# First block's attention: where VectorE does a finished branch's product and sum, and when ScalarE copies the first factor

## The reference

```python
Kc = compress(kc_raw, pe_k, ck_w1, ck_w2)
Vc = compress(vc_raw, pe_v, cv_w1, cv_w2)
...
s_c = jnp.einsum('bgrtd,bgnd->bgrtn', qblk, Kc) - slope * dist_c
p_c = jnp.where(valid_c, jax.nn.softmax(jnp.where(valid_c, s_c, NEG), axis=-1), 0.0)
o_c = jnp.einsum('bgrtn,bgnd->bgrtd', p_c, Vc)
...
p_s = jax.nn.softmax(s_s, axis=-1).reshape(B, G, R, T, n_sel, SEL_BLOCK)
o_s = jnp.einsum('bgrtnl,bgtnld->bgrtd', p_s, Vsel)
...
p_w = jax.nn.softmax(jnp.where(valid_w, s_w, NEG), axis=-1)
o_w = jnp.einsum('bgrts,bgsd->bgrtd', p_w, vwin)
return gblk[..., 0:1] * o_c + gblk[..., 1:2] * o_s + gblk[..., 2:3] * o_w
...
x = x + jnp.concatenate([m_out, a_out], axis=-1) @ w_out[i]
x = x + conv_ffn(rms_norm(x, ln2_g[i]), w_up[i], conv_w[i], conv_b[i], w_down[i])
```

## Time and profile before

| | |
|---|---|
| median of 3 runs | 1676.45 us (1676.28 to 1678.82) |
| profiled execution | 1674.83 us, span 1673.5 us |
| mean granted TensorE clock | 0.985 |
| PE busy | 1606.2 us (96%), 10381 matmuls |
| DVE busy | 871.9 us (52%) |
| ACT busy | 633.4 us (38%) |
| POOL busy | 50.4 us (3%) |
| in 217 to 355 us: PE, DVE, ACT busy, clock | 121.06, 79.79, 75.54 of 138 us, 0.90 |

### The profile page before, as it was taken

The page is one execution under the profiler, slowest core; times in us unless marked ns, Lnnn a source line. Parts: engine busy times, 40 slices in busy tenths (PEclk is TensorE's granted clock), DMA queues, the critical chain, the costliest instruction groups (busy, mean ns, idle before and its releaser), DMA issues.

```text
span 1673.5 us, 24837 instructions
## 1 busy us (share of the span) xinstructions
PE 1606.2 (96%) x10381; PEld 1356.3 (81%) x10381; DVE 871.9 (52%) x1558; ACT 633.4 (38%) x1124; POOL 50.4 (3%) x51
## 2 busy tenths in 40 slices
PE   7999978999999999999999999999999998999997
PEld 5898766677888888899888778999987887678886
DVE  4434666556644655855454455436555445545443
ACT  5232256443322334733344342223333343442333
POOL 0000001000000000020000000000020000000000
PEclk9999989899999999999999899999999999999999
DMA  6234400024233322332112102223422113113231
GB/s 196 76 80 89 113 14 14 14 88 119 84 100 101 101 80 96 99 67 76 51 51 49 54 14 77 77 89 120 96 51 76 51 37 51 54 39 101 89 113 51
DMA packets 175600, 125.22 MB, mean 75 GB/s; under 512 B 48752, under 2 KB 172272, under 8 KB 175488
## 3 DMA queue, kind: packets, MB, share of 16 engines
q1 hardware_dynamic: 175488, 123.63, 26.5%
HBM read 121.52 MB, written 2.10 MB: 74 GB/s over the span
## 4 chain that ended last, share of the span: by engine, by line
PE 89%; DVE 4%; ACT 4%; issue 2%; DMA 1%; SPq 0%; POOL 0%; DVEq 0%; ACTq 0%; POOLq 0%
PE bank L586 69%; PE bank L2743 2%; PE bank L2775 2%; PE bank L2755 2%; PE bank L3151 1%; ACT w_hi L533 1%; PE bank L2651 1%; PE bank L2602 1%; PE bank L1602 1%; DVE w_lo L542 1%; PE bank L1658 1%; PE bank L3114 1%; PE bank L1478 1%; ACT probs L1532 1%; PE bank L3130 1%
## 5 line engine op out<-in xcount | busy, mean ns | idle before, releaser
L586 PE MATMUL bank<-h_hi,w_hi 128*128 128x512 f32 (+2 forms) x920 | 327.4, 376 | 7.6 <-issue 4.4
L542 DVE TENSOR_TENSOR w_lo<-w_raw,w_hi 128x2048 fp32r<-128x2048 f32 (+2 forms) x117 | 241.2, 2061 | 177.0 <-ACT w_hi L533 176.4
L586 PE MATMUL bank<-h_lo,w_hi 128*128 128x512 f32 (+2 forms) x920 | 322.6, 370 | 0.0
L586 PE MATMUL bank<-h_hi,w_lo 128*128 128x512 f32 (+2 forms) x920 | 321.2, 369 | 0.0
L533 ACT ACTIVATE w_hi<-w_raw 128x2048 fp32r<-128x2048 f32 (+2 forms) x117 | 201.1, 1719 | 74.4 <-DMA w_raw<-w_in 36.0
L586 PEld LDWEIGHTS bank<-h_hi,w_hi 128*128 128x128 f32 (+1 forms) x920 | 166.9, 189 | 49.9 <-issue 16.6
L586 PEld LDWEIGHTS bank<-h_hi,w_lo 128*128 128x128 f32 (+1 forms) x920 | 166.6, 189 | 30.6 <-issue 0.2
L586 PEld LDWEIGHTS bank<-h_lo,w_hi 128*128 128x128 f32 (+1 forms) x920 | 166.5, 189 | 30.1 <-issue 0.5
L586 PE MATMUL bank<-g_hi,w_hi 128*128 128x264 f32 (+1 forms) x752 | 183.0, 309 | 1.4 <-DVE z_a L2225 0.9
L586 PE MATMUL bank<-g_lo,w_hi 128*128 128x264 f32 (+1 forms) x752 | 180.8, 306 | 0.0
L586 PE MATMUL bank<-g_hi,w_lo 128*128 128x264 f32 (+1 forms) x752 | 180.4, 306 | 0.0
(11 more groups left out here) (574 smaller groups left out, 2633.1 us busy)
## 6 DMA issues: line engine op xcount, KB each, us to landing
w_raw<-w_in SPq DMA_DIRECT2D x45, 1024.0 KB, 5.3
w_raw<-w_up SPq DMA_DIRECT2D x32, 512.0 KB, 4.9
w_raw<-w_in SPq DMA_DIRECT2D x40, 256.0 KB, 4.5
w_raw<-w_down SPq DMA_DIRECT2D x8, 1024.0 KB, 5.1
w_raw<-w_out SPq DMA_DIRECT2D x8, 1024.0 KB, 5.1
w_raw<-w_out SPq DMA_DIRECT2D x8, 512.0 KB, 3.4
w_raw<-w_ple_gate SPq DMA_DIRECT2D x4, 1024.0 KB, 5.1
w_raw<-w_o_attn SPq DMA_DIRECT2D x8, 512.0 KB, 3.5
```

Of the source, the lines that this page charges most:

```text
L542: DV.e.tensor_tensor(wlo[u % RING][:, 0:n], raw[u % RING][:, 0:n], whi[u % RING][:, 0:n].bitcast(F32), ALU.subtract).then_inc(*w_low(u))
L586: ins = PE.e.matmul(out, stationary[a](k), moving[b](k)[i], start=first and n == 0, stop=last and n == 2)
```

## The change

Two edits. In `nsa_steps`, used by ScalarE and VectorE, the value part of unit step - 3 moves ahead of the step's fill. In `ac_nsa_turn` the copy of the first unit's factor (unit (0, 0, 0)) moves from the second unit's turn, at step 3, to the end of the first unit's own turn at step 2, behind its `ac_nsa_wide` and ahead of the exponentials of unit (0, 2, 0), which ScalarE does in the same step. TensorE's order is not changed.

```diff
@@ -1614,7 +1614,7 @@
         def ac_nsa_turn(unit):
             i = number_n[unit]
             dst, src = flip(unit, 0)
-            if i and is_last(units_n[i - 1]):
+            if i > 1 and is_last(units_n[i - 1]):
                 ac_nsa_factors(units_n[i - 1])
             if i > 1:
                 AC.wait_ge(*n_valued.at(i - 2))
@@ -1622,6 +1622,7 @@
             AC.e.activation(dst, src, ACT.Copy).then_inc(*n_flip_a(i, 0))
             if i == 0:
                 ac_nsa_wide(unit)
+                ac_nsa_factors(unit)
 
         def ac_nsa_widen(unit):
             i = number_n[unit]
@@ -1736,11 +1737,11 @@
                 for stage_, behind in stages_:
                     if 0 <= step - behind < len(units_n):
                         stage_(units_n[step - behind])
+                if step > 2:
+                    value(units_n[step - 3])
                 while given < 11 * min(step, len(units_n)) // len(units_n):
                     next(fill)
                     given += 1
-                if step > 2:
-                    value(units_n[step - 3])
 
         def ac_nsa():
             fence(AC, "mlstm")
```

## The result

| | before | after |
|---|---|---|
| median | 1676.45 us (3 runs: 1676.28, 1676.45, 1678.82) | 1663.05 us (4 runs: 1659.98, 1662.26, 1663.84, 1665.06) |
| ratio | | 0.9919, 95% interval 0.9899 to 0.994 |
| profiled execution, span | 1674.83, 1673.5 us | 1663.84, 1662.5 us |
| mean granted TensorE clock | 0.985 | 0.992 |

A fourth run of before was disturbed (3445.82 us) and is neither in the median nor in the ratio. By the ratio the change is faster by 0.8%, some 13.6 us (10 to 17); a second comparison of the same two kernels gave 10.8 us (experiment 5). The forecast of 1663.0 agrees with the median to 0.1 us. That is closer than its steps deserve: the stalls came out as worked out, the clock gave less, the first factor more, and what lies outside the stage differed too.

What follows compares the result with a forecast made beforehand. TensorE was taken as the bound, carrying 89% of the chain. Stalls 5.06, clock 7.8 and first factor 0.6 sum to 13.5 us off the profiled 1674.83; from the median 1676.45 that gives 1663.0 us, range 1658 to 1670.

Steps and rivals of the forecast that it cites:

- The order of the code: In nsa_steps, fill and finished branch meet on VectorE only at steps 15, 19 and 24; the swap acts nowhere else.
- B: Step 19, unit (2,2,3): TensorE's stall of 0.83 us goes; called the tightest spot of the three.
- Part 1: VectorE's product moves ahead of addition and split at three places; TensorE's stalls go, 5.06 us together.
- the prediction's last part: Signs expected in the trace after, among them w_lo still waiting for w_hi, with about 0.4 us.
- A: Step 15, unit (2,1,3): TensorE's stall of 2.28 us for the finished branch goes.
- C: Step 24, unit (3,1,3): TensorE's stall of 1.95 us for the finished branch goes.
- Part 2: TensorE's three low-clock stretches in or behind the stalls all go: 7.8 us, bounds 0 to 7.8.
- rival (a): A low-clock stretch stays or appears, or VectorE's probsT copy replaces B's wait: 1666 to 1669.2 us; chance 27%.
- Part 3: In the opening, ScalarE copies the first factor ahead of eight exponentials: 0.6 us gained, between +1.0 and -1.6.
- (b): Only the stalls go and every low-clock stretch lasts as now: 5.7 us gained, 1670.8 us; chance 8%.
- (c): VectorE's multiply is late in its new place and TensorE stalls elsewhere: 1674 to 1676.5 us; chance 4%.
- (d): Slower: shifted later TensorE gaps bring new low-clock stretches, 3.1 us each; five give 1678.5 us; chance 3%.

Runs made afterwards that it cites:

- experiment 5: The kernel after, unchanged, run once more against the kernel before: 1664.39 us, ratio 0.9933.
- experiment 4: Kernel before, with the branch's product and sum put between the dense step's addition to X and its split; first factor as before: 1666.83 us, ratio 0.9942.
- experiment 10: Kernel with late copies, and at B ScalarE's w_hi also held back behind that place's second factor: 1659.76 us, one execution.
- experiment 3: Kernel before, with 16, 6 and 14 useless identity transposes on TensorE ahead of its waits at A, B and C: 1670.47 us, ratio 0.997.
- experiment 2: Kernel before with only the earlier copy of the first factor, without the swap in nsa_steps: 1674.54 us, ratio 0.999.
- experiment 6: Kernel before with value ahead of the fill only at step 19 (place B): 1674.36 us, ratio 0.9996.
- experiment 7: Kernel after, with 4 to 8 more identity transposes on TensorE in each of its waits for a branch factor: 1664.96 us, ratio 0.9941.
- late copies: Kernel after, with ScalarE's first, second and fourth mLSTM fill copies held back behind the next step's branch factor: 1660.29 us, ratio 0.9909.
- experiment 1: Kernel after without the two edits in ac_nsa_turn, so the swap in nsa_steps alone: 1663.4 us, ratio 0.9928.

## Why the prediction was right, and where it was not

**The order of the code** (steps 15, 19 and 24 and no others): right. The dense step from X7 to X8, which has no finished branch beside it, stayed at 6.99 us, and the swap at B alone took away B's stall alone.

**Part 1, the stalls**: right in size and cause. 2.28 + 0.83 + 1.95 = 5.06 us were predicted; 2.34 + 0.96 + 2.03 = 5.33 measured. The cover named for the moved instructions, the wait for `w_hi`, is there, and it is the split that had held them up (experiment 4). Of it the prediction's last part expected 0.4 us to be left; measured were 0.24 us at B and nothing at A and C, so the cover is just used up, as its own starts (288.4 against 288.39) had said. The product's starts were given to 0.1 us against the stage. That B is the tightest place was right, and experiment 10 shows no slack there.

**Part 2, the clock**: the mechanism was right (experiment 3), and 7.8 us against 7.63 is right for the profiled execution of before. (The eight transposes from which the share of 0.46 comes are of 128x128 each, not of 128x512; the share stays.) Wrong was the step that took the clock as safe afterwards, with the patch of 246 to 250 us as its evidence. After contains the same patch:
```profile
249.77 0.66 PE L1602 MATMUL bank<-identity,probs 128*128 128x128 f32 x4 [1.31 <-ACT branch_factor L1560]
```
Here low clock follows it at 252. In before, and in the second execution of after, the same wait has no low clock behind it:
```profile
248.69 0.66 PE L1602 MATMUL bank<-identity,probs 128*128 128x128 f32 x4 [1.31 <-ACT branch_factor L1560]
```
```profile
248.40 0.65 PE L1602 MATMUL bank<-identity,probs 128*128 128x128 f32 x4 [1.31 <-ACT branch_factor L1560]
```
A thin patch that kept the clock once is no proof that it keeps it. Here the mechanism of rival (a) came true, though not its time, with 39.46 - 36.33 = 3.13 us at the two stretches. The same holds for the stalls: their clock cost was 7.63 us in one execution and 3.1 in experiments 2 and 6 (two stretches each, A and B or A and C). The rule that I set against myself, from the Trainium skill, "TensorE: Matmul & The Clock Gate", section "The HAM clock gate", says that what watches the engine runs free of the kernel's start. These traces agree: equal gaps at equal places of the stage are followed by the low clock in one execution and not in the next. The phase itself no trace shows.

**Part 3, the first factor**: 0.6 us were predicted at once, 1.48 came by the second factor, and nothing is left at the first addition to X in experiments 2 and 5, each with one low stretch behind the opening that takes 1.5 us. The lines of the opening after, answering:
```profile
231.63 0.60 ACT L1560 ACTIVATE branch_factor<-bank 128x512 f32<-128x512 f32 x1 [0.81 <-PE bank L1541]
...
235.72 0.58 ACT L1622 ACTIVATE probsT<-bank 128x512 f32<-128x512 f32 x1
...
237.69 0.69 DVE L1641 COPY probsT<-bank 128x512 f32<-128x512 f32 x1
...
239.58 0.58 ACT L1560 ACTIVATE branch_factor<-bank 128x512 f32<-128x512 f32 x1
...
240.22 0.66 PE L1602 MATMUL bank<-identity,probs 128*128 128x128 f32 x4 [1.12 <-ACT branch_factor L1560]
```
ScalarE's wait for TensorE's transposes is 0.81 us where I had said 1.2: I had taken their end from a row of 0.89 us, part of which ran at the low clock. The copies of `probsT` on ScalarE and VectorE come 0.4 us earlier against the stage, not at the same time. So the term was mis-sized: 1.48 for 0.6 in the opening, then minus 1.5 us of clock, which the lower bound of -1.6 foresaw. A low stretch that begins between F2 and X1 stands in all three executions with the early copy and no other edit on ScalarE or TensorE (two of them in after), and in one of the six with the old first factor. Whether the early copy brings them or chance does is open; a net gain from it at X1 shows only together with the transposes of experiment 7 (54.82 us from S, 56.01 in before) or the late copies (52.14).

**The sum.** Of the 13.5 us: stalls 5.33 instead of 5.06, clock 7.63 - 3.13 = 4.5 instead of 7.8, first factor 1.48 instead of 0.6; together 11.3, which is the stage's 11.31. The median moved by 13.4 because its shift also holds the luck of the rest of the kernel, within an interval of 7 us. The agreement of the totals to 0.1 us is chance; what the working supports is the range of 1658 to 1670.

**Rivals.** (b), only the stalls: out by experiments 1 and 3. (c), the product late in its new place: out, the product starts right behind TensorE's products. (d), five new stretches: not seen. Three to eight stretches stand outside the stage in every trace, before's included, and those behind the stage move its time by up to 6 us. That is the mechanism of (d), at some 1.3 to 1.5 us for each 3.4 us of low clock, but it works both ways and the two executions of the kernel after differ by it too.

## What to carry to other kernels

An instruction that another engine waits for should not stand behind one that itself waits for a third engine: on VectorE the product needed 0.7 us and stood 2.5 us behind `w_lo`'s wait for `w_hi`. Count such a stall with the clock that it costs behind it, but as a range: here the same three stalls were worth 5.3 us themselves and between 3.1 and 7.6 us of clock. Where a kernel's executions spread by more than the change is worth, compare stages from mark to mark in the trace; pieces without low clock repeated to 0.05 us.

## What was not expected of the hardware

Useless work on TensorE paid: 16, 6 and 14 transposes put into stalls kept the granted clock at 1.00 through 69 us and made the kernel 0.3% faster. In the opening, on the other hand, more low clock cost nothing that can be seen, while ScalarE is the bound: in the swap alone TensorE ran 13.70 us at half clock there, in before 10.24, and S to F2 was 19.68 us in both. In the kernel after it was 18.20 us in both executions, with 6.8 and with 3.4 us of low clock. No execution had none there, so its whole price isn't known.
```profile
226.50:240.20 13.70, 11.66 (x65) 0.51 0.00 1
```
